# Choosing and fetching experts in sixteen blocks (one token half of one head each) instead of eight, with twelve row buffers

## The reference

```python
def peer_ffn(xn, wq, subkeys, u_tab, v_tab):
    q = (xn @ wq).reshape(b, s, PEER_HEADS, 2, PEER_HALF)      # 8 heads
    sc = einsum('bshjc,hjkc->bshjk', q, subkeys)               # 128 scores for each of 2 halves
    top_s, top_i = lax.top_k(sc, PEER_TOPK)                    # 16 best of each
    cand = top_s[..., 0, :, None] + top_s[..., 1, None, :]
    best, ci = lax.top_k(cand, PEER_TOPK)                      # 16 best pairs
    idx = i1 * PEER_N_KEYS + i2                                # 16 experts for each token and head
    g = jax.nn.softmax(best, axis=-1)
    act = gelu(einsum('ckd,cd->ck', u_tab[ic], xc))            # 128 experts for each token
    return einsum('ck,ckd->cd', (gc * act), v_tab[ic])
```

## Time and profile before

| | us |
|---|---|
| median of 3 runs (2376.75 to 2386.36) | 2380.74 |
| the profiled execution: its own time | 2378.23 |
| the profiled execution: span from first to last instruction | 2376.4 |
| PE busy | 1884.7 (79%) |
| DVE busy | 1445.1 (61%) |
| POOL busy | 937.3 (39%) |
| ACT busy | 817.5 (34%) |
| mean granted TensorE clock | 0.918 |

### The profile page before, as it was taken

One profiled execution on the slowest core, in us unless ns is written; L12 is line 12 of the kernel. 1 busy time (PEld: TensorE's weight loads), 2 busy tenths in 40 slices (PEclk: granted clock), 3 DMA queues, 4 the chain that ended last, 5 costly groups with the idle time before them and its releaser, 6 DMA issues. The chain is left out here.

```text
span 2376.4 us, 22813 instructions
## 1 busy us (share of the span) xinstructions
PE 1884.7 (79%) x7348; PEld 1158.5 (49%) x7348; DVE 1445.1 (61%) x3034; ACT 817.5 (34%) x2247; POOL 937.3 (39%) x908
## 2 busy tenths in 40 slices
PE   7978588688777777898867886878777767698797
PEld 7846455233222222685654532322222237598797
DVE  7685755876454444676576478645444456498642
ACT  4231123343333333423212334433333344344221
POOL 4585213344333333457721243433333325066230
PEclk9959799889999999996888997999999989799898
DMA  5434677999999999443458699999999943243001
GB/s 208 144 106 168 255 283 288 421 421 421 422 421 421 421 421 421 180 156 108 152 204 317 249 422 421 421 421 422 421 422 421 421 180 131 81 151 133 1 1 45
DMA packets 107688, 660.93 MB, mean 278 GB/s; under 512 B 11952, under 2 KB 13360, under 8 KB 41648
## 3 DMA queue, kind: packets, MB, share of 16 engines
q0 software_dynamic: 73728, 536.90, 54.9%
q1 hardware_dynamic: 33840, 122.56, 15.0%
HBM read 658.37 MB, written 1.05 MB: 277 GB/s over the span
## 5 line engine op out<-in xcount | busy, mean ns | idle before, releaser
L570 PE MATMUL banks<-big 128*128 128x512 f32 x1680 | 824.5, 626 | 268.9 <-ACT big L755 268.5
L1070 DVE SCALAR_TENSOR_TENSOR big<-big,banks 128x1024 bf16<-128x1024 f32 x420 | 507.1, 1220 | 423.5 <-DMA big<-in_experts,big 422.1
L832 POOL DMA_INDIRECT big<-in_experts,big x420 | 395.4, 942 | 768.7 <-PE banks L570 708.1
L570 PEld LDWEIGHTS banks<-big 128*128 128x128 f32 x1680 | 305.9, 195 | 775.1 <-ACT big L755 495.7
L747 ACT ACTIVATE big<-big 128x1 f32<-128x1 f32 x512 | 102.3, 200 | 624.2 <-DVE big L1070 622.6
L755 ACT ACTIVATE big<-constants,big 128x128 f32<-128x128 f32 x512 | 205.5, 401 | 80.6 <-PE banks L570 37.9
L570 PE MATMUL banks<-expert_rows,big 128*128 128x512 f32 x368 | 179.6, 617 | 42.7 <-ACT big L755 42.7
L1070 DVE SCALAR_TENSOR_TENSOR big<-expert_rows,banks 128x1024 bf16<-128x1024 f32 x92 | 111.8, 1220 | 115.8 <-DMA expert_rows<-in_experts,big 115.8
L1360 PE MATMUL banks<-x_parts,chunk_parts 128*128 128x256 f32 x1152 | 150.1, 294 | 26.9 <-POOL chunk_parts L1350 26.9
L1360 PEld LDWEIGHTS banks<-x_parts,chunk_parts 128*128 128x128 f32 x1152 | 147.3, 201 | 28.8 <-POOL chunk_parts L1350 12.6
L751 ACT ACTIVATE big<-big 128x1 f32<-128x1 f32 x512 | 150.7, 294 | 17.8 <-ACT big L747 0.4
(11 more groups left out here) (351 smaller groups left out, 2273.4 us busy)
## 6 DMA issues: line engine op xcount, KB each, us to landing
big<-in_ada SPq DMA_DIRECT2D x48, 512.0 KB, 4.2
weight_ring<-in_w_in SPq DMA_DIRECT2D x40, 512.0 KB, 4.3
weight_ring<-in_wq SPq DMA_DIRECT2D x32, 512.0 KB, 3.5
weight_ring<-in_gdn_in SPq DMA_DIRECT2D x32, 512.0 KB, 3.3
weight_ring<-in_w_out SPq DMA_DIRECT2D x16, 640.0 KB, 3.9
weight_ring<-in_lru_in SPq DMA_DIRECT2D x16, 512.0 KB, 3.4
big<-in_experts,big POOLq DMA_INDIRECT x420, 22.6
weight_ring<-in_w_kv SPq DMA_DIRECT2D x8, 512.0 KB, 4.7
```

The source lines that it names most:

```text
L570: last = nc.tensor.matmul(sums_e[tt][:, c * 512:(c + 1) * 512], diag[:, v % NDIAG], rows_e[v % NBUF][:, D + c * 512:D + (c + 1) * 512], st ...
L832: nc.gpsimd.indirect_dma_start(rows_e[v % NBUF], None, d_e, bass.IndirectOffsetOnAxis(ap=expert[:, h, tt, a:a + 1], axis=0)).then_inc(arri ...
L1070: nc.vector.scalar_tensor_tensor(waste[:, v % 2], rows_e[v % NBUF][:, 0:D], 1.0, x_rows[tt], ALU.mult, ALU.mult, accum_out=dots[:, v:v + 1 ...
```

## The change

A block `g` is one head of one token half: `g = 8 * tt + head`, 16 blocks a layer, in the order in which the units use them. Scores, choice, decode, exponential and gates are done for each block instead of for each head.

- Heads 0 to 3 (instead of 0 to 2) are scored ahead of the units. Blocks 0 and 1 are chosen and decoded there, as before, but for the first token half alone.
- ACT copies a head's scores in two pieces: the first token half into `score`, the second into `score_late`, where it is kept for all eight heads until its block comes.
- The query tiles of heads 4 to 7 come one at a time, after units 8 and 14 of each run of 16, the scores after unit 16.
- DVE calls `choose(g + 1, g)` after unit 16(g - 1) - 8 and `decode(g)` four units later, for g = 2 to 15, so up to unit 220. ACT's exponential comes two units after the decode, DVE's gates eight after it.
- The key scores of head 0 stand ahead of the transposes of x on PE; the transposes for the second token half move from unit 28 to unit 104.
- Smaller arrays (a ring of two for ranks and candidates, `dots` overwritten by gelu and by its product) make room for a twelfth row buffer.

```diff
-NBUF = 11
+NBUF = 12
-EARLY_HEADS = 3
-TILES_AT = {3 + 4 * i: EARLY_HEADS + i for i in range(PH - EARLY_HEADS)}
+EARLY_HEADS = 4
+GROUPS_E = NT * PH
+TILE_AT = {TOPK * (h - EARLY_HEADS) + 8 + 6 * j: 2 * h + j for h in range(EARLY_HEADS, PH) for j in range(2)}
...
+CHOICE_AT = {TOPK * (g - 1) - 8: g for g in range(2, GROUPS_E)}
+DECODE_AT = {at + 4: g for at, g in CHOICE_AT.items()}
...
-TURN_X_AT = 28
+TURN_X_AT = SLOTS - 24
...
     query_tile(1)
+    pe.wait_ge(s("sub_loaded"), 32)
+    key_scores(0)
     pe.wait_ge(s("out_added"), KD)
     turn_x(0)
-    pe.wait_ge(s("sub_loaded"), 32)
-    key_scores(0)
...
-    nc.scalar.copy(score[:, h % 4], nc_ps[2 + h % 2][:, :]...).then_inc(s("score_kept"), 1)
+    ps_ = nc_ps[2 + h % 2][:, :].rearrange("p (t a c) -> p t a c", t=NT, a=2)
+    nc.scalar.copy(score[:, h % 4], ps_[:, 0]).then_inc(s("score_early"), 1)
+    nc.scalar.copy(score_late[:, h], ps_[:, 1]).then_inc(s("score_kept"), 1)
...
-    for h in range(EARLY_HEADS - 1):
-        best_exp(h)
+        if h in (1, 3):
+            best_exp(h // 2)
...
-    if v % TOPK == 0 and tt == 0:
-        pool.wait_ge(s("experts_ready"), h + 1)
+    if a == 0:
+        pool.wait_ge(s("experts_ready"), g + 1)
...
     choose(0, None)
     choose(None, 0)
     decode(0)
     choose(1, None)
+    gates(0)
     choose(2, 1)
     decode(1)
-    gates(0)
     gates(1)
     for v in range(UNITS):
         dot(v)
         if v in CHOICE_AT:
-            a = CHOICE_AT[v]
-            choose(a if a < PH else None, a - 1)
-            decode(a - 1)
+            g = CHOICE_AT[v]
+            choose(g + 1 if g + 1 < GROUPS_E else None, g)
+        if v in DECODE_AT:
+            decode(DECODE_AT[v])
```

More of the change, by code:

```diff
@@ L211, in first_block @@
     query = r(4, T)
-    score = r(4, NT * 2, NK)
-    spare = r(NT * 2, NK)
-    topf = r(PH, NT, 2, TOPK)
+    score = r(4, 2, NK)
+    score_late = r(PH, 2, NK)
+    spare = r(2, NK)
+    topf = r(RING, 2, TOPK)
     dots = r(UNITS)
[L216 to L231, removed]
+    cand = r(RING, NCAND)
+    cand2 = r(NCAND)
+    top = r(RING, 2, TOPK)
+    topi = r(RING, 2, TOPK).bitcast(U32)
+    best = r(RING, TOPK)
+    besti = r(RING, TOPK).bitcast(U32)
+    ex = r(GROUPS_E, TOPK)
+    gate = r(GROUPS_E, TOPK)
+    row = r(TOPK).bitcast(U32)
+    second_row = r(TOPK)
+    column = r(TOPK)
+    pickf = r(2, TOPK)
+    key = r(2, TOPK)
+    gsum = r(GROUPS_E)
+    expert = r(GROUPS_E, TOPK).bitcast(U32)
+    diag = r(NDIAG, P)
+    waste = r(2, D // 2).bitcast(BF16)
+    assert r.at <= KD * KD * P
     r = Region(big, XN_AT)
@@ L234, in first_block @@
     sub = r(2 * PH, NK)
-    expert = r(PH, NT, TOPK).bitcast(U32)
-    diag = r(NDIAG, P)
-    waste = r(2, D // 2).bitcast(BF16)
     rows_e = [r(ROW) for _ in range((XN_AT - r.at) // ROW)] + mem_["rows"]
     assert len(rows_e) == NBUF
-    hit = Region(work, 4 * T)(NT * 2 * TOPK, TOPK)
-    out_e = [score.rearrange("p m i t -> p (m i t)")[:, tt * D:(tt + 1) * D] for tt in range(NT)]
+    hit = Region(work, 4 * T)(2 * TOPK, TOPK)
+    out_e = [query.rearrange("p m t -> p (m t)"), score.rearrange("p m i t -> p (m i t)")]
     base = big[:, C_BASE:C_BASE + 1]
@@ L826, in _ @@
                 for v in range(UNITS):
[L827 to L829 removed]
+                    tt, g, a = unit(v)
+                    if a == 0:
+                        pool.wait_ge(s("experts_ready"), g + 1)
                     if v >= NBUF:
                         pool.wait_ge(s("down_done"), v - NBUF + 1)
[L832 removed]
+                    nc.gpsimd.indirect_dma_start(rows_e[v % NBUF], None, d_e, bass.IndirectOffsetOnAxis(ap=expert[:, g, a:a + 1], axis=0)
                                                  ).then_inc(arrived(f"rows_loaded{v % NBUF}"), 16)
@@ L1011, in choose @@
                     if a is not None:
-                        dve.wait_ge(s("score_kept"), a + 1)
-                        ranked += [(top[:, a, i // 2, i % 2], topi[:, a, i // 2, i % 2], score[:, a % 4, i], spare[:, i]) for i in range(2 * NT)]
+                        ra, late, ha = a % RING, a // PH, a % PH
+                        dve.wait_ge(s("score_kept" if late else "score_early"), ha + 1)
+                        source = score_late[:, ha] if late else score[:, ha % 4]
+                        ranked += [(top[:, ra, j], topi[:, ra, j], source[:, j], spare[:, j]) for j in range(2)]
                     if b is not None:
-                        ranked += [(best[:, tt, b], besti[:, b, tt], cand[:, b % 2, tt], cand2[:, tt]) for tt in range(NT)]
+                        rb = b % RING
+                        ranked += [(best[:, rb], besti[:, rb], cand[:, rb], cand2)]
                     for v, at_, x, y in ranked:
@@ L1022, in choose @@
                     link(last)
-                    if a is not None:
+                    if a is not None and not late:
                         dve.sem_inc(s("score_used"), 1)
```

84 lines of the change are left out of this document (40 added, 44 removed).

## The result

The changed kernel takes 2319.86 us (median of 4 runs, 2319.17 to 2324.99) against 2383.41 us before. The ratio is 0.9742, 95% interval 0.9715 to 0.9769. On another chip it was 0.9723 (0.9710 to 0.9736). So it is faster by 2.6 to 2.8%, where 3.6% were forecast. The time lies above the forecast's own range (2281 to 2306), and just inside the end of 2320 that was taken for the first rival. The profiled execution took 2320.48 us, its span is 2318.5 us, 57.9 less than before instead of 87.3 less.

The account below looks back on a forecast made before the run. The DMA bounds the gather stages once it runs; removing idle time saves 37.3 and 37.6 us, earlier fetches 12.4, together 87.3: 2378.2 becomes 2290.9, stated as 2294 us. Own range 2281 to 2306, extended to 2320 for the first rival.

Parts of the forecast that it names:

- the first rival: First four groups of a layer: PE and ACT bind at 48 us a group, 8.6 us lost a layer, 2311 us; chance 0.10.
- the sum: Gather stages of 655.8 and 656.8 us, 37.3 and 37.6 less; with 12.4 from earlier first fetches, 87.3 us less.
- What bounds the kernel: Gather stages: DMA bounds once running; engines waiting for each other round tile pairs leave 39.8 us idle in layer 0.
- The heads among the units: First four groups of 16 units: PE needs 43.1 us, DMA 42.7; 0.4 over each, 1.6 absorbed by 13 us in hand.
- First unit: Start of a gather stage: PE's first unit done by 283.3 us, 13 us in hand, 2.9 gone if PE starts slow.
- Start: Before the first fetch: choice takes 8.3 us for 14.0, first fetch 6.2 us earlier, 12.4 us over both layers.
- The later groups: Ranking past unit 128 in each gather stage: choices hidden behind over 20 us of fetches in flight, cost 0.
- signs of being wrong: Gather stages: DMA share under 0.95, dots over 2.52 us apart, granted clock under 0.8; unit 12's fetch expected by 285.
- The low clock: PE in gather stages: gaps at 14 choices keep the clock low; at 0.6, 2456 us, slower than before; chance 0.03.

Follow-up runs that it names:

- the first experiment: The changed kernel with the exponential after unit 13 instead of 14: 2308.07 us, ratio 0.9712 to the kernel before.
- the last two runs: Changed kernel with the exponential ahead of the tile copy: 0.9684; kernel before with the new order alone and the exponential after unit 13: 0.9684.

## Why the prediction was right or wrong

The direction was right and so was what the change removes; the size was not, chiefly because one term of the sum was too small: 57.9 us less in the profiled execution instead of 87.3. The 29.4 us that are missing lie as follows. The stages are 12.2 and 9.5 us longer than the sum had them (668.0 and 666.3 for 655.8 and 656.8). Of these 21.7 us the first experiment, in which the dips are gone, gives back 13.7. The other 8.0 it keeps (659.6 and 661.0), some 3.6 of them by the longer step of the dots (2.517 and 2.525 us for 2.512 and 2.516), the rest unexplained. The starts lack 5.2, and the part behind the last dot is 2.2 longer (455.7 us for 453.5), which is within the spread of the profiles (452.9 to 457.6). So about half of the miss is the step that failed. With it mended the best kernels reach 0.968, still not the 0.964 that was forecast.

- *What bounds the kernel.* Right. The hole of 39 us a layer was the engines waiting for each other round pairs of tiles, and the new order alone removes most of it (0.9778). That the long choices had a share in it holds for the old order alone, where halving them, with the twelfth buffer, saved 9 us of the 39; with the order changed, their length makes no difference to the blocks or the deficit.
- *The heads among the units.* This is the step that failed: "That is 43.1 us. The DMA needs [...] 42.7. PE is a hair slower in these four groups, 0.4 each, and the 13 us in hand absorb 1.6." Measured were 45.6 us. The sum had every wait and every instruction, and even the two table loads on PE's path. It did not have what such a wait does to PE: after 4.33 us idle two units took 5.18 to 6.52 us instead of 3.46, on average 2.2 of the 2.5 us that lack. The text priced that fall of the clock once, at the start, and gave it a rival of its own, but only at the scale of a whole stage. It is paid in each of four blocks. There 2.9 us a block against the DMA make 11.6 us, where 1.6 were allowed. Moving the exponential by one unit, and nothing else, takes the blocks to 42.3 us or less in layer 0 and 43.1 or less in layer 1, and the dips away, which shows the term.
- *The average hid the worst point.* From unit 8 to 15 PE has both tiles, both waits and the exponential and only eight units, 8 x 1.73 + 2 x 3.6 + 1.39 + 4.33 + 1.7, some 28.5 us, for which the DMA needs 8 x 2.512 + 2.5 = 22.6. In the eight units that follow it gains only 3 of these 6 back. So some 6 us of what is in hand are needed inside a block, whatever its total. Comparing block totals could not show that, and the dips begin at such a point (POOL's 10.63 us at 423.58).
- *First unit.* 13 us in hand were forecast from a first unit 23.3 us behind the first fetch; it was 27.9 in the first profile: 3 with a stall that not every execution has, the rest from a slow start for which the text had allowed 2.9.
- *Start.* The work was halved as computed (8.6 us, forecast 8.3). The first fetch moved 3.0 and 4.1 us in this pair of profiles, instead of 6.2. The run-up varies: in the nine profiles of kernels with blocks it came between 256.7 and 264.8 us, 262.4 on average, against 266.3, 266.1 and 271.1 in the three with choices for both halves, 267.8 on average. From the last dot of layer 0 to the next fetch it is 264.1 on average (259.1 to 268.6) against 269.7. So the term is 5.4 and 5.6 us on average, near its 6.2; that this pair of profiles shows less is the spread.
- *The later groups.* Right: cost nothing, shown by leaving them out (659.0 to 659.2 us against 659.6 to 661.0).
- *The rivals.* PE and ACT binding in the first four groups is what happened, from 45.6 us instead of the 48 it named, and it was given 0.10. Its condition, blocks 2.9 us over the DMA, was one slow pair of units away from the sum. That the measured 2319.86 lies within the 2320 taken for this rival is luck: the rival came to its time by other numbers, blocks of 48 us with 13 us in hand. Two of the text's own signs of being wrong did come, a DMA share of 0.85 and 0.79 and a thirteenth fetch later than 285 us. The low clock did not come as a rule of the whole stage (granted 0.90 to 0.96). In the four blocks, though, each wait of 4.33 us is followed by units at 1.2 GHz. So the Trainium skill (TensorE: Matmul & The Clock Gate, HAM oscillation), which describes repeated waits that send the clock back down each time, was right for the blocks, and the trace agrees with its 0.53 from 374.4 us.

## What to carry to other kernels

Where two chains are within a few per cent of each other, compare them at the worst point inside a period, not over the period, and price the slow matmuls after each wait of some microseconds. Look for an activation table load on the path of a copy that another engine waits for: moving it by one unit was worth as much here (0.9723 to 0.9689 or 0.9679 on one chip) as the division into blocks and the twelfth buffer that the change brought (0.9778 to 0.9742, on two chips). And before smaller pieces are blamed or praised, run the new order alone: with it and the moved exponential, the old choices for both halves reach 0.9684 as well.

## What the runs showed of the hardware

- PE's clock behind short waits, in the blocks with tiles. After a wait of 4.32 to 4.34 us for ACT the units that followed ran at 0.5 of the clock, in all 32 cases of four profiles. After 2.80 us it was so in four cases of eight, and after 1.39 and 1.94 us with one unit between in five of eight. After single waits of 1.3 to 1.7 us it never was, in over 200 cases. A slow unit costs 1.7 us. So at the waits in between, the length of the wait alone does not say whether the clock falls, and equal kernels can differ by it from layer to layer.
- A stall of 2.5 us on DVE and 6.6 us on ACT, ending within 0.14 us of each other, while the DMA was at its full rate, in both layers of the first profile of the changed kernel (the second 1.8 and 5.9 us), not in its second profile, and again in both profiles of the chip of the last two runs. The instruction queues moved a packet of 8 KB at 274.7 us, in the middle of it; the profile of the changed kernel without the stall has such a packet too, at 275.5 us, as long after its first fetch. Whether the engines waited for instructions was not tested.
- In the long quiet part of a gather stage most fetches land 2.485 us apart, and a few steps are 0.97 us longer. The kernel before has three of them from dot 132 to 252 in each layer. Each follows an 8 KB instruction packet by about 2 us (packets at 657.1 and 762.4 us, long steps ending at 659.2 and 764.6), but four more such packets of layer 0 are followed by none. They are why a fetch costs 2.51 and not 2.49 us. Kernels with blocks have four in layer 0 and five in layer 1, where the landings can be followed, and a mean step of 2.517 to 2.519 and 2.522 to 2.526 us (the first profile of the changed kernel 2.517 in both). Without the late ranking it was four and four, 2.516 us in both. That the packets make the long steps, and that the length of the program makes their number, stays open.
- Loads from HBM ran at 420 to 422 GB/s wherever nothing held the fetches back. The Trainium skill (DMA: Bandwidth & Descriptors, Where 436 GB/s comes from) has the HBM side bind a load at some 358, its figure for each core, and names beside it a measured 425 that is near the rate of the fabric. The measurement here, on one core, disagrees with the first and is close to the second, and it decides.
